# Two transformer blocks in one kernel on one core: the root steps of h3's tiles taken in pairs, v's passes waiting by halves of a tile, and both first k blocks ahead of tiles 2 and 3

## The reference

```python
def rms_norm_2(x, g):
    xf = x.astype(jnp.float32)
    y = xf * lax.rsqrt(jnp.mean(xf * xf, axis=-1, keepdims=True) + EPS)
    return (y * g.astype(jnp.float32)).astype(x.dtype)

y = gmlp_mixer(...)                    # its last step is y @ w_out (a_w_out)
h = h + rms_norm_2(y, a_post_g[i])
kv_in = rms_norm_2(h, kv_norm_g)
k_shared = (kv_in @ w_k).reshape(bsz, s_len, N_KV_HEADS, HEAD_DIM)
v_shared = (kv_in @ w_v).reshape(bsz, s_len, N_KV_HEADS, HEAD_DIM)
...
q, z = jnp.split(rms_norm_2(h, b_pre_g[j]) @ w_in, 2, axis=-1)
```

## Time and profile before

| | |
|---|---|
| median of 3 runs | 886.77 us (886.73 to 887.48) |
| the profiled execution | 887.39 us |
| its span, first to last instruction | 885.7 us |
| TensorE busy | 869.7 us, 98% |
| GpSimd busy | 543.0 us, 61% |
| VectorE busy | 536.4 us, 61% |
| ScalarE busy | 360.6 us, 41% |
| granted TensorE clock over the span | 1.000 |
| TensorE busy from 660 to 690 us | 24.79 of 30 us |
| GpSimd busy from 670 to 690 us | 19.18 of 20 us |

### The profile page before, as it was taken

One profiled execution on the slowest core, in us unless ns is written; L12 is line 12 of the kernel. 1 busy time (PEld: TensorE's weight loads), 2 busy tenths in 40 slices (PEclk: granted clock), 3 DMA queues, 4 the chain that ended last, 5 costly groups with the idle time before them and its releaser, 6 DMA issues.

```text
span 885.7 us, 11936 instructions
## 1 busy us (share of the span) xinstructions
PE 869.7 (98%) x4220; PEld 722.6 (82%) x4220; DVE 536.4 (61%) x880; ACT 360.6 (41%) x804; POOL 543.0 (61%) x604
## 2 busy tenths in 40 slices
PE   8999999999999999999999999999998999999997
PEld 6888888888888787878888888888887888888876
DVE  6125647875035589765765635556996457788624
ACT  4123333431125277547112321112775536666622
POOL 7766646586789832217976038771359798566352
PEclk9999999999999999999999999999999999999999
DMA  7533231342322368995652262525962222112202
GB/s 197 167 120 96 76 91 48 96 143 81 134 96 95 121 141 172 212 211 191 154 132 95 62 200 87 128 95 141 222 183 72 72 73 87 56 49 72 73 1 95
DMA packets 81516, 102.65 MB, mean 116 GB/s; under 512 B 11825, under 2 KB 54321, under 8 KB 81458
## 3 DMA queue, kind: packets, MB, share of 16 engines
q1 hardware_dynamic: 72752, 85.12, 29.8%
q0 software_dynamic: 8704, 16.78, 11.2%
q10 hardware_dynamic: 2, 0.00, 0.0%
HBM read 99.79 MB, written 2.10 MB: 115 GB/s over the span
## 4 chain that ended last, share of the span: by engine, by line
PE 88%; POOL 4%; DVE 2%; ACT 2%; DMA 2%; issue 1%; POOLq 0%; DVEq 0%; ACTq 0%
PE bank L2075 26%; PE bank L2077 26%; PE bank L2076 26%; PE bank L2318 2%; PE bank L2172 1%; PE bank L2346 1%; DMA gain<-in_a_w_in 1%; DVE wlo L1666 1%; POOL wlo L849 1%; PE bank L2291 1%; PE bank L2341 1%; PE bank L2340 1%; DMA raw<-in_a_w_in 1%; POOL whi L840 1%; POOL ms L794 1%
## 5 line engine op out<-in xcount | busy, mean ns | idle before, releaser
L849 POOL TENSOR_TENSOR wlo<-raw,whi 128x512 fp32r<-128x512 f32 x204 | 280.6, 1406 | 0.7 <-ACT whi L971 0.7
L840 POOL TENSOR_SCALAR whi<-raw 128x512 fp32r<-128x512 f32 x202 | 141.2, 736 | 187.6 <-PE bank L2077 179.1
L2075 PE MATMUL bank<-actB_hi,whi 128*128 128x512 f32 (+1 forms) x416 | 159.5, 384 | 0.6 <-POOL wlo L849 0.6
L2076 PE MATMUL bank<-actB_lo,whi 128*128 128x512 f32 (+1 forms) x416 | 158.6, 381 | 0.0
L2077 PE MATMUL bank<-actB_hi,wlo 128*128 128x512 f32 (+1 forms) x416 | 158.5, 381 | 0.0
L2075 PE MATMUL bank<-whi,actA_hi 128*128 128x512 f32 x318 | 125.9, 396 | 1.5 <-DVE actA_lo L1420 0.7
L2077 PE MATMUL bank<-whi,actA_lo 128*128 128x512 f32 x318 | 123.9, 390 | 0.0
L2076 PE MATMUL bank<-wlo,actA_hi 128*128 128x512 f32 x318 | 123.9, 390 | 0.0
L2075 PEld LDWEIGHTS bank<-actB_hi,whi 128*128 128x128 f32 x416 | 78.3, 188 | 15.6 <-issue 1.0
L2077 PEld LDWEIGHTS bank<-actB_hi,wlo 128*128 128x128 f32 x416 | 78.2, 188 | 15.1
L2076 PEld LDWEIGHTS bank<-actB_lo,whi 128*128 128x128 f32 x416 | 78.3, 188 | 14.2
(11 more groups left out here) (269 smaller groups left out, 1580.0 us busy)
## 6 DMA issues: line engine op xcount, KB each, us to landing
raw<-in_a_w_in SPq DMA_DIRECT2D x44, 512.0 KB, 4.0
raw<-in_w_in SPq DMA_DIRECT2D x32, 512.0 KB, 3.9
raw<-in_b_w_in SPq DMA_DIRECT2D x16, 512.0 KB, 3.3
raw<-in_a_w_out SPq DMA_DIRECT2D x12, 512.0 KB, 3.3
gain<-in_a_w_out POOLq DMA_DIRECT2D x9, 512.0 KB, 8.5
raw<-in_w_out SPq DMA_DIRECT2D x8, 512.0 KB, 4.0
raw<-in_w_ple_gate SPq DMA_DIRECT2D x8, 512.0 KB, 3.3
gain<-in_a_w_in POOLq DMA_DIRECT2D x8, 512.0 KB, 8.0
```

The lines of the kernel that those rows point to most:

```text
L840: pool.tensor_scalar(H, src[:, i * HALF:(i + 1) * HALF], 1.0, 1.0, ALU.mult, ALU.mult).then_inc(w_hi, 1)
L849: ins = pool.tensor_tensor(L, src[:, i * HALF:(i + 1) * HALF], H.bitcast(f32), ALU.subtract)
L2075: M(out_, whi_, xhi_, start=start, stop=False)
L2076: M(out_, whi_, xlo_, start=False, stop=False)
```

## The change

1. GpSimd: a new function `root_two` takes two tiles' roots: two sums of 128x1, then one power of 128x2. It replaces `root("a", 0)` and `root("a", 1)` at their place, and `root("a", 2)` and `root("a", 3)`, which stood between the two L840 and the two L849 instructions of k5's second half and behind that half; the pair stands behind that half. `root("h3", 2)` moves from there to between L840 and L849 of q5's first half, where `root("h3", 3)` was, and that one goes between the two L849 instructions.
2. TensorE: both first k blocks, ("Fa", "k5", 0) and ("Fa", "k5", 1), stand ahead of the transposes of tile 2; before, the second of them stood between those of tile 2 and tile 3.
3. TensorE: v5 of a tile waits for the first half of `rest_n` only, and for the second ahead of k = 4.
4. ScalarE: the two copies of v5's first results move ahead, one ahead of `h3_out(2)`, one ahead of `normed_n(2)`, and `h3_out(3)` stands behind `normed_n(2)` as before. VectorE: `part_gain(3, 0)` moves ahead of `h3_in(2)`, so that `h3_in(2)` and `h3_in(3)` stand together.

```diff
     o += turn("n", 0) + turn("n", 1) + [("v5", 0), ("v5", 1)]
-    o += [("Fa", "k5", 0)] + turn("n", 2) + [("Fa", "k5", 1)] + turn("n", 3)
+    o += [("Fa", "k5", 0), ("Fa", "k5", 1)] + turn("n", 2) + turn("n", 3)
...
+            def root_two(name, t):
+
+                n = NORMS[name]
+                for u in (t, t + 1):
+                    nth = next(roots)
+                    pool.wait_ge(squared[name], T + u + 1)
+                    pool.tensor_scalar(ms[:, n, u:u + 1], ss[:, n, u, 0:1], ss[:, n, u, 1:2], EPS, ALU.add,
+                                       ALU.add).then_inc(ms_ready, 1)
+                pool.wait_ge(ms_ready, nth)
+                pool.tensor_tensor(rstd[:, n, t:t + 2], ms[:, n, t:t + 2], mhalf[:, 0:1].to_broadcast([P, 2]), ALU.pow)\
+                    .then_inc(rstd_ready[name], 2)
...
-            after[at("v5", 0, 1) - 0.25] = [lambda: root("a", 0, D), lambda: root("a", 1, D)]
+            after[at("v5", 0, 1) - 0.25] = [lambda: root_two("a", 0)]
             after[at("v5", 0, 1)] = [lambda: root("h3", 0, D)]
             after[at("k5", 0, 0) - 0.5] = [lambda: root("h3", 1, D)]
-            after[at("k5", 0, 1) - 0.5] = [lambda: root("a", 2, D)]
-            after[at("k5", 0, 1)] = [lambda: root("a", 3, D), lambda: root("h3", 2, D)]
-            after[at("q5", 0, 0) - 0.5] = [lambda: root("h3", 3, D)]
+            after[at("k5", 0, 1)] = [lambda: root_two("a", 2)]
+            after[at("q5", 0, 0) - 0.5] = [lambda: root("h3", 2, D)]
+            after[at("q5", 0, 0) - 0.25] = [lambda: root("h3", 3, D)]
...
             square_a(3, 0)
+            v5_out(0)
             h3_out(2)
+            v5_out(1)
             normed_n(2)
-            v5_out(0)
             h3_out(3)
-            v5_out(1)
             normed_n(3)
...
             rest_n(1)
+            part_gain(3, 0)
             h3_in(2)
-            part_gain(3, 0)
             h3_in(3)
...
                 if kind == "v5":
-                    pe.wait_ge(lo["n"], 2 * (s + 1))
+                    pe.wait_ge(lo["n"], 2 * s + 1)
...
                     for k in range(KD):
+                        if k == 4:
+                            pe.wait_ge(lo["n"], 2 * t + 2)
```

## The result

The changed kernel took **890.62 us** (median of 6 runs, 890.03 to 891.57), the kernel before beside it 886.79: a ratio of 1.0040, with a 95% interval of 1.0030 to 1.0049, or **+3.8 us**. The forecast was 888.4, with 889.9 as the upper end of its range. So it was wrong: the sign of its sum held, the size did not, and the time lies above the range. The profiled execution took 890.03, of which 888.3 is span (887.39 and 885.7 before). It can be compared stage by stage, and the stages are where the prediction put them.

The account below looks back on a forecast made before the run. TensorE's waits for GpSimd's queue of roots bound the kernel, measured at v5's start of tile 2. Tile 2's root +2.7, shorter way to normed_n(3) -0.5, halves -0.6: +1.6 us, giving 888.4; range 886.4 to 889.9.

Parts of the forecast that it names:

- What bounds the kernel: TensorE, busy 98% of the span; its waits hang on GpSimd's roots, measured by v5's start of tile 2 at 689.67.
- I take it one to one: From v5 of tile 2 to the kernel's end: the +1.6 us delay there reaches the end in full.
- The first pair: a's roots, tiles 0 and 1: GpSimd waits 2 us, h3's root of tile 1 +0.5; -0.2 at v5, not reaching the end.
- Halves: v5's passes on TensorE: waiting for only the first half of rest_n starts them 0.6 us sooner.
- The second pair: a's roots, tiles 2 and 3, behind k5's splits on GpSimd: h3's root of tile 2 comes at 685.1 instead of 682.41.
- R2: Time when both of a's roots for tiles 2 and 3 are ready on GpSimd: 679.65 (679.2 to 680.1).
- rival 2: Tile 2's root stays at 682.4, so the shorter way and the halves give -1.1: 885.7; chance 0.08.
- The price c: Lengthening of GpSimd's q5 scalings beside VectorE's h3_in: 1.3 us from gate-stage rows, bounds 0 to 2.4.
- rival 1: GpSimd and VectorE don't get in each other's way, c below 0.6: +0.3 to +0.9, about 887.3; chance 0.14.
- From h3's root of tile 2 to v5: ScalarE, GpSimd and TensorE steps from that root at 685.1 to v5 of tile 2 at 691.3.
- the term for the clock: TensorE's 3 us idle between the transposes of tiles 2 and 3: no clock loss counted in the sum.
- rival 3: Clock falls to half rate behind TensorE's hole between tiles 2 and 3, costing 1.8 more: +3.4, 890.2; chance 0.06.

Follow-up runs that it names:

- number 7: Kernel before with the change's halves and k order, a's pair for tiles 2 and 3 inside k5's second half, h3's roots and squares earlier; 884.73 us.
- number 10: Kernel before with the pair of tiles 2 and 3 ahead of k5's last subtractions, plus 10 filler passes ahead of tile 0's transposes; 884.69 us.
- number 4: Changed kernel with 16 filler passes ahead of tile 0's transposes and 16 between those of tiles 2 and 3; 889.66 us.
- number 2: Kernel before with only a's roots for tiles 0 and 1 paired by root_two; 888.12 us, ratio 1.0008.
- number 1: Kernel before with only v5 waiting for the first half of rest_n, and for the second ahead of k = 4; 886.41 us, ratio 0.9993.
- number 3: Kernel before with v5's waits by halves and both first k blocks ahead of tile 2's transposes, roots as before; 887.31 us, ratio 0.9998.
- number 11: Changed kernel with single roots for a's tiles 0 and 1, as before the change; 890.10 us, ratio 1.0038.
- number 12: Changed kernel with h3's root of tile 2 right behind a's pair of tiles 2 and 3, ahead of q5's scalings; 890.08 us, ratio 1.0039.
- number 5: Kernel before with only a's roots for tiles 2 and 3 paired, plus the h3 root places and ScalarE and VectorE orders belonging to it; 889.83 us.
- number 8: Changed kernel with tile 3's squares (h3_out(3)) ahead of normed_n(2) on ScalarE; 887.96 us, ratio 1.0015.
- number 6: Kernel before with 10 filler passes ahead of tile 0's transposes and 8 ahead of tile 2's, the latter into a bank still in use; 888.70 us.

## Why the prediction was wrong

**What bounds the kernel**: right. v5's start of tile 2 was the measure: in number 7, where it came 2.15 earlier, 2.0 reached the end (2.13 and 2.1 in number 10); in number 4, where the clock stayed up, +2.44 there is +2.4 in the median. "I take it one to one" holds where the clock does; where it falls behind v5's start, the end moves by more (+2.83 and +3.8 in the changed kernel).

**The first pair**: the mechanism was right, the size too small. GpSimd waited 2.22 (2 forecast). But h3's root of tile 1, put at 671.05, came at 671.50 (+0.93 for +0.48). The pair's own end was late by 0.47 (664.67 for 664.2), and all later steps with it. The power was right: 0.73 for an estimate of 0.72. The two sums were not: the prediction gave them no time of their own, only a start of the power at 663.4. They took 3.12 beside four VectorE instructions (1.37 and 0.80 before, apart), and the power started at 663.94. Number 2 shows the term by itself: 0.89 at every later root, +0.9 in the median.

**Halves**: right by the traces (0.6 in numbers 1 and 3); the medians don't settle it, 0.8 earlier in number 1 with an interval that reaches no change, and no gain in number 3.

**The second pair**: R2 came at 680.17 for 679.65, all of it from the first pair (679.27 without it, in number 11, for 679.17 by the prediction's steps). That the splits set it, and not the squares, was right; rival 2 is dead.

**The price c**: 1.6 for 1.3. Its sign and its place were right, so rival 1 is dead; the gate stage's rows were the right neighbour, a fifth too cheap. One reading against rival 1 was wrong: not every GpSimd instruction beside h3_in was lengthened. v5lo's subtraction took 1.29 beside h3_in(1) and 1.28 beside h3_in(0) now, where such a subtraction takes 1.27 with VectorE idle (688.87); there VectorE paid, 2.46 for 1.40.

**From h3's root of tile 2 to v5**: 692.11 - 685.97 = 6.14 in number 4, for 6.2. Right.

**The sum of the chain**: R2 +0.52, c and rounding +0.3 and the rest -0.06 make the forecast's +1.6 a **+2.4**, which is number 4's trace and median. That is within the forecast's own range (up to +3.1).

**The step that failed is the term for the clock, put at nothing in the sum**, with a chance of 0.06 for rival 3 and an upper end of the range that didn't reach over it. Number 4 shows it at 1.4 by the medians, 0.94 by the traces; on top of the chain's +2.4 it makes the +3.8, while the chain alone, about 889.2, lies inside the range. The prediction had named the place (between the transposes of tiles 2 and 3), the idle time (about 3 us; 2.58 measured), the sight (eight transposes at half rate; 1.94 measured against 1.91 at the kernel's start) and the time (890.2; 890.6 measured). What spoke against it was one row: the last matmul at 880 and the clock below 1.00 only from 884 on, read as a clock that outlives 4 us of idle time. But the row shows a fall that comes late, and no passes behind it that could have met it. The falls came late here too: in number 12 about 4.3 us and in number 5 about 5.2 us behind the last matmul ahead of the hole, when the hole was already over; in the changed kernel 2.0. That the row does not carry over is shown by four kernels (the changed one, 5, 11 and 12); why the delay differs is not shown. The size of the rival was somewhat high (1.8 on top of the chain, for 1.4 or 0.94), and the chain under it was low; that the two errors nearly cancel in 890.2 is luck. The Trainium skill (TensorE: Matmul & The Clock Gate, Why this matters for your kernels) has the warning that a gap between bursts sends the clock back; the trace agrees for this gap, 0.50 in the two microseconds behind its 2.58, while number 12 kept 1.00 behind one of 2.34. The hole was certain by the forecast's own steps and only its effect was open, so the range had to reach over it.

The smaller error is in the chain: +2.4 for +1.6, from the two sums of the first pair and from c.

What stays open is the split between chain and clock to better than about a microsecond: +2.4 and +1.4 rest on intervals of about 0.8 us to each side.

## What to carry to other kernels

A change that gathers waits into one hole on TensorE is to be priced with the clock: where the forecast itself makes a hole of the length seen here (2.6 us beside eight transposes), a lower clock behind it belongs in the forecast. Pairing steps saves one short instruction and makes the first of the pair wait for the second; on a queue without a gap the whole queue inherits that wait, so look for the place where the pair can stand *earlier* (number 7) before it is put where the later member stood.

## What the hardware showed that was not expected

- **The same idle time does not always bring the clock down.** In the profiled executions 2.34 ahead of tile 0's transposes was followed by transposes at half rate at once (number 2; number 8 after 2.32) or only in tile 1's (the changed kernel), and by none in number 12, where eight transposes took 1.06 and the clock was 1.00 from 672 to 674. On the other side it fell in number 3 after 1.65 and 0.80 and in number 1 after 1.82, and not in number 11 after 1.61. The 2.58, 2.59, 3.87 and 3.95 between or ahead of the transposes of tiles 2 and 3 were followed by a fall in all four kernels; in number 5 it came only after the transposes.
- **A fall costs nothing where another wait takes it in.** Between 670 and 678 the clock fell in four of the kernels. In number 2 the waits ahead of tile 1's transposes and of v5 took it in; in the changed kernel the wait ahead of tile 2's transposes (0.31, for 1.60 in number 4); in numbers 3 and 8 tile 2's transposes started without a wait, and 1.07 and 0.76 were still left ahead of tile 3's. In number 8 the clock was 0.50 to 0.72 from 670 to 676, and v5 of tile 2 still started 1.8 before that of the changed kernel.
- **GpSimd's one-column instructions are drawn out beside VectorE instructions with two inputs in SBUF**, the sums most: 0.29 undisturbed, 3.12 for two beside four such instructions. The power keeps to 0.56 or 0.57 in four of the eight roots of the kernel before and takes 0.84 to 1.40 in the others. Beside rest_n, with one input in PSUM (674.09 to 675.36), the sum at 674.76 stays at 0.30. A two-column power takes 0.73 where VectorE is idle, and 0.97 in number 7 beside the end of a part_gain.
- **A filler has a queue position too**: in number 6 eight passes that compute nothing waited 1.89 for their bank, and the kernel came out 1.5 us slower by its ratio, 2.0 by the medians.
